# First feed-forward block: down products with the weights moving, output by token, turned back by 16 transposes

## The reference

```
def conv_ffn(xn, w_gate, conv_w, conv_b, w_up, w_down):
    S = xn.shape[1]
    g = xn @ w_gate
    gp = jnp.pad(g, ((0, 0), (CONV_WIDTH - 1, 0), (0, 0)))
    gc = conv_b + sum(conv_w[j] * gp[:, j:j + S] for j in range(CONV_WIDTH))
    h = jax.nn.gelu(gc, approximate=False) * (xn @ w_up)
    return h @ w_down
...
    for i in range(DEPTH):
        hn = rms_norm(h, norm_mix[i])
        ...
            mix = mla_mixer(hn, b_w_in[j], b_q_norm[j], b_w_uq[j], b_kv_norm[j], b_w_ukv[j], b_w_o[j], cos_r, sin_r)
        h = h + mix.astype(h.dtype)
        f = conv_ffn(rms_norm(h, norm_ffn[i]), ffn_w_gate[i], ffn_conv_w[i], ffn_conv_b[i], ffn_w_up[i], ffn_w_down[i])
        h = h + f.astype(h.dtype)
    return rms_norm(h, norm_final)
```

## Time and profile before

| | us |
|---|---|
| median of 3 runs (1070.09 to 1070.32) | 1070.15 |
| the profiled execution's own time | 1069.82 |
| its span | 1068.0 |
| PE busy in the span | 1059.3 (99%) |
| DVE, ACT, POOL busy | 746.9, 599.0, 142.3 |
| granted TensorE clock | 1.0 of full speed (2.4 GHz) throughout |

### The profile page before, as it was taken

The page is one execution under the profiler, slowest core; times in us unless marked ns, Lnnn a source line. Parts: engine busy times, 40 slices in busy tenths (PEclk is TensorE's granted clock), DMA queues, the critical chain, the costliest instruction groups (busy, mean ns, idle before and its releaser), DMA issues.

```text
span 1068.0 us, 18604 instructions
## 1 busy us (share of the span) xinstructions
PE 1059.3 (99%) x7388; PEld 911.8 (85%) x7388; DVE 746.9 (70%) x1274; ACT 599.0 (56%) x1021; POOL 142.3 (13%) x166
## 2 busy tenths in 40 slices
PE   9999999999999999999999999999999999999998
PEld 7887878656898999799999899899998798888886
DVE  5665565487555878868875887686777767777775
ACT  4532666544434567766565656555574556555464
POOL 0000010153110000623431100000022410000000
PEclk9999999999999999999999999999999999999999
DMA  9731121286613342056444364545542334544551
GB/s 384 321 140 64 74 79 40 89 287 219 223 53 119 125 156 86 2 198 228 157 168 138 139 227 168 197 160 196 180 175 98 141 119 157 198 175 186 212 184 52
DMA packets 25381, 168.69 MB, mean 158 GB/s; under 512 B 3280, under 2 KB 3536, under 8 KB 5456
## 3 DMA queue, kind: packets, MB, share of 16 engines
q1 hardware_dynamic: 25152, 167.25, 43.3%
q10 hardware_dynamic: 144, 0.26, 0.1%
HBM read 164.35 MB, written 1.05 MB: 155 GB/s over the span
## 4 chain that ended last, share of the span: by engine, by line
PE 97%; ACT 1%; DVE 1%; issue 0%; DVEq 0%; ACTq 0%
PE bank L438 19%; PE bank L440 18%; PE bank L439 18%; PE bank L444 15%; PE bank L445 8%; PE bank L1557 2%; PE bank L501 2%; PE bank L1721 2%; PE bank L1711 2%; PE bank L1701 1%; PE bank L1584 1%; PE bank L1575 1%; PE bank L453 1%; PE bank L2370 1%; PE bank L1402 1%; ACT TILE L1760 1%
## 5 line engine op out<-in xcount | busy, mean ns | idle before, releaser
L416 DVE TENSOR_TENSOR wlo<-raw,whi 128x1024 fp32r<-128x1024 f32 (+1 forms) x255 | 303.7, 1237 | 67.8 <-ACT whi L401 67.7
L438 PE MATMUL bank<-OPS,whi 128*128 128x256 f32 (+1 forms) x1012 | 320.1, 316 | 0.2
L440 PE MATMUL bank<-OPS,wlo 128*128 128x256 f32 (+1 forms) x1012 | 312.0, 308 | 0.0
L439 PE MATMUL bank<-OPS,whi 128*128 128x256 f32 (+1 forms) x1012 | 311.9, 308 | 0.0
L401 ACT ACTIVATE whi<-raw 128x1024 fp32r<-128x1024 f32 (+1 forms) x255 | 255.5, 1052 | 57.9 <-PE bank L440 55.4
L444 PE MATMUL bank<-OPS,whi 128*128 128x512 f32 x704 | 250.1, 399 | 0.2
L438 PEld LDWEIGHTS bank<-OPS,whi 128*128 128x128 f32 x1012 | 192.7, 190 | 17.1 <-issue 5.6
L440 PEld LDWEIGHTS bank<-OPS,wlo 128*128 128x128 f32 x1012 | 192.8, 191 | 9.8
L439 PEld LDWEIGHTS bank<-OPS,whi 128*128 128x128 f32 x1012 | 192.9, 191 | 9.6 <-issue 1.2
L445 PE MATMUL bank<-OPS,wlo 128*128 128x256 f32 x704 | 197.7, 281 | 0.0
L444 PEld LDWEIGHTS bank<-OPS,whi 128*128 128x128 f32 x704 | 132.3, 188 | 32.9 <-DVE FIRST L2599 0.8
(11 more groups left out here) (294 smaller groups left out, 1299.2 us busy)
## 6 DMA issues: line engine op xcount, KB each, us to landing
raw<-in_stream SPq DMA_DIRECT2D x143, 1024.0 KB, 4.9
PROJ<-in_stream SPq DMA_DIRECT2D x5, 1024.0 KB, 18.5
raw<-in_stream SPq DMA_DIRECT2D x4, 1056.0 KB, 8.5
PROJ<-PROJ SPq DMA_DIRECT2D x32, 64.0 KB, 3.7
FIRST<-in_first SPq DMA_DIRECT2D x1, 1248.0 KB, 5.5
C<-in_con SPq DMA_DIRECT2D x1, 1157.5 KB, 7.4
FIRST<-in_first SPq DMA_DIRECT2D x1, 1024.0 KB, 7.5
WST<-in_w_s SPq DMA_DIRECT2D x2, 256.0 KB, 7.8
```

What stands on the lines that cost most here:

```text
L416: nc.vector.tensor_tensor(c.w[1][:, part], c.raw[:, part], c.w[0][:, part].bitcast(F32), ALU.subtract).then_inc(*raises(c.lo[h]))
L438: nc.tensor.matmul(out, w[0], x[0], start=start, stop=False, skip_group_check=skip)
L439: nc.tensor.matmul(out, w[0], x[1], start=False, stop=False, skip_group_check=skip)
L440: return nc.tensor.matmul(out, w[1], x[0], start=False, stop=stop, skip_group_check=skip)
```

## The change

In block 0 `narrow` is gone, and `by_token` makes the down products there too: 24 matmuls of 512 columns per chunk in place of 48 of 256. Its banks are filled in the order 0, 2, 1, 3, without the opening transposes of X. The output now lies by token, and X by feature, so it has to be turned back. In `copy_rows` ScalarE copies each finished bank to SBUF (`rows_out`, four copies of 128 x 512). In `turn_rows` TensorE makes eight transposes of 128 x 128 from two of these copies into two of the banks; the first eight stand in down 10 ahead of its last bank, the other eight behind the first feature block of the latents (`amid`, called in `together` after k = 0). VectorE adds the turned banks to X, in pairs.

```diff
@@ Jobs.pe_step
                     for k in range(KD):
                         for j in i:
                             self.product.fill_part(e, self.product.jobs[j], (k,))
+                        if k == 0 and self.product.amid is not None:
+                            self.product.amid(e)
@@ ffn
-            def narrow(e, c, ch):
-                for point in due(e, ch.lo, ("h_hi_made", l, c), ("h_lo_made", l, c)):
-                    e.wait_ge(*point)
...
-                for f in range(KD):
-                    for t in range(2):
-
-                        mm = products(acc[f // 2].mem[:, (f % 2) * SEQ:(f % 2 + 1) * SEQ],
-                                      tuple(w[:, t * D + f * P:t * D + (f + 1) * P] for w in ch.w),
-                                      (HH[c % 2][:, t, :], HL[c % 2][:, t, :]),
-                                      c == 0 and t == 0 and f % 2 == 0, c == NF - 1 and t == 1, skip=True)
-                    if c == NF - 1 and f in (1, 3, 5):
-                        mm.then_inc(*raises(("sum_given", l, f // 2)))
-                mm.then_inc(*raises(ch.used))
+            rows_out = [PROJ[:, 512 * i:512 * i + 512] for i in range(4)]
+            pair_bank = [acc[2 * (m % 2) + m // 2] for m in range(4)]
+
+            def turn_rows(e, half):
+                for m in (2 * half, 2 * half + 1):
+                    for point in due(e, ("rows_copied", l, half), ("rows_copied", l, half + 2)):
+                        e.wait_ge(*point)
+                    for b in range(2):
+                        at = P * (2 * (m % 2) + b)
+                        for t in range(2):
+                            mm = nc.tensor.transpose(pair_bank[m].mem[:, b * SEQ + t * P:b * SEQ + t * P + P],
+                                                     rows_out[half + 2 * t][:, at:at + P], ident)
+                    mm.then_inc(*raises(("rows_turned", l, m)))
+
+            def copy_rows(e, i):
+                for point in due(e, given[i]):
+                    e.wait_ge(*point)
+                nc.scalar.activation(rows_out[i], acc[i].mem[:], ACT.Copy).then_inc(*raises(("rows_copied", l, i)))
@@ by_token
-                    for i, a in enumerate(acc):
+                    for i, a in enumerate(acc if l else ()):
...
-                for i, a in enumerate(acc):
+                for i in (0, 1, 2, 3) if l else (0, 2, 1, 3):
+                    a = acc[i]
+                    if l == 0 and c == NF - 1 and i == 3:
+                        turn_rows(e, 0)
@@ act of ffn
                 split_hi(e, by["down", NF - 1].s + 2.5)
+                for i in (0, 2, 1, 3) if l == 0 else ():
+                    copy_rows(e, i)
                 for i in range(1, 4 if l == 0 else 1):
                     s.gives.act(e, (2 * i - 2, 2 * i - 1))
@@ dve of ffn
-                for i, a in enumerate(acc if l == 0 else ()):
-                    for point in due(e, given[i]):
+                if l == 0:
+                    split_lo(e, by["down", NF - 1].s + 2.5)
+                for m, a in enumerate(pair_bank if l == 0 else ()):
+                    for point in due(e, ("rows_turned", l, m)):
                         e.wait_ge(*point)
-                    x = X[:, 2 * i:2 * i + 2, 0:SEQ]
+                    x = X[:, 2 * m:2 * m + 2, 0:SEQ]
                     nc.vector.tensor_tensor(x, two(a.mem), x, ALU.add).then_inc(*raises(a.read["dve"]))
-                    if i == 0:
-                        split_lo(e, by["down", NF - 1].s + 2.5)
-                    else:
-                        s.gives.dve(e, (2 * i - 2, 2 * i - 1))
-                    if i == 1:
+                    if m == 1:
+                        s.gives.dve(e, (0, 1))
                         split_lo(e, by["down", NF - 1].s + 3)
+                        s.gives.dve(e, (2, 3))
+                    if m == 3:
+                        s.gives.dve(e, (4, 5))
@@ program
         la = mla_latent(op1.block, high)
+        la.amid = ff.turn_rest
```

More of the change, by code:

```diff
@@ L1204, in dve @@
                         s.gives.dve(e, range(2 * i - 2 if i > s.begun else 0, 2 * i))
-            s.gives = s.after_act = None
+            s.gives = s.after_act = s.amid = None
             s.pe, s.act, s.dve = pe, act, dve
@@ L2875, in add_halves @@
                     *raises(("halves_summed", l, c, what)))
-            def narrow(e, c, ch):
-                for point in due(e, ch.lo, ("h_hi_made", l, c), ("h_lo_made", l, c)):
-                    e.wait_ge(*point)
-                if c == 0:
-                    for point in due(e, [a.empty for a in acc]):
-                        e.wait_ge(*point)
-                for f in range(KD):
-                    for t in range(2):
-                        mm = products(acc[f // 2].mem[:, (f % 2) * SEQ:(f % 2 + 1) * SEQ],
-                                      tuple(w[:, t * D + f * P:t * D + (f + 1) * P] for w in ch.w),
-                                      (HH[c % 2][:, t, :], HL[c % 2][:, t, :]),
-                                      c == 0 and t == 0 and f % 2 == 0, c == NF - 1 and t == 1, skip=True)
-                    if c == NF - 1 and f in (1, 3, 5):
-                        mm.then_inc(*raises(("sum_given", l, f // 2)))
-                mm.then_inc(*raises(ch.used))
+            rows_out = [PROJ[:, 512 * i:512 * i + 512] for i in range(4)]
[12 more added lines that the diff above has]
+                for point in due(e, given[i]):
+                    e.wait_ge(*point)
+                nc.scalar.activation(rows_out[i], acc[i].mem[:], ACT.Copy).then_inc(*raises(("rows_copied", l, i)))
             def by_token(e, c, ch):
@@ L2908, in by_token @@
                         w = tuple(w[:, at:at + 512] for w in ch.w)
-                        mm = products(a.mem[:], (HH[c % 2][:, t, tokens], HL[c % 2][:, t, tokens]), w, False,
-                                      c == NF - 1 and t == 1, skip=True)
+                        mm = products(a.mem[:], (HH[c % 2][:, t, tokens], HL[c % 2][:, t, tokens]), w,
+                                      l == 0 and c == 0 and t == 0, c == NF - 1 and t == 1, skip=True)
                     if c == NF - 1 and i < 3:
@@ L2937, in pe @@
                         wide(e, up[c], ch)
-                    elif l == 0:
-                        narrow(e, c, ch)
                     else:
@@ L3072, in ffn @@
             s.acc, s.given = acc, given
-            s.block = lambda k: acc[k // 2].freed
+            s.block = lambda k: pair_bank[k // 2].freed
+            s.turn_rest = lambda e: turn_rows(e, 1)
             s.used = [("down_added", l, NF - 1)]
```

## The result

| | before | with the change |
|---|---|---|
| median, us | 1070.16 (20 runs, 1069.87 to 1070.83) | 1071.62 (20 runs, 1071.18 to 1073.0) |
| ratio to before | | 1.0014 (95% interval 1.0008 to 1.0021) |
| span of the profiled execution, us | 1068.0 | 1069.4 |

The changed kernel is 1.46 us slower, 0.14%, which is clear of zero and under the 0.2% that the prediction calls no change. The forecast was +0.97.

A forecast was written before the change was run, and what follows sets the result against it. TensorE, 97% of the chain, was taken as the bound. The terms -2.86 - 0.10 + 1.87 + 1.94 + 0.12 gave +0.97 us, so 1071.1 us on the median, 0.09% slower; range 1069.1 to 1072.4.

The forecast's parts named there:

- if it waits again before their end: Sign of being wrong: TensorE, after the one wait ahead of the first latent matmul, waits again before the latents end.
- The products: Block 0's down stages fall from 5.76 to 5.50 us, 0.26 per chunk over 11 chunks: -2.86 us.
- gate and up: Block 0's gate and up stages, 11.31 us against block 1's 11.29: taken as -0.10 us, bounds -0.2 to 0.
- The transposes: Sixteen added on TensorE at 0.104 us each, 1.71, plus 0.16 for two slower first products: +1.87 us.
- Rival (c): Each of the 16 transposes costs its whole duration of 0.272 us: +2.64, or 1073.7 us; chance 2%.
- The new wait: TensorE idles ahead of the first latent matmul because ScalarE's high part queues behind all four copies: +1.94 us, bounds 0 to 2.3.
- rival (a): No wait ahead of the latents, whose first block is ready when down 10 ends: -0.97, or 1069.2 us; chance 8%.
- Down 10's start: From down 9 to down 10 in block 0, HL of chunk 10 comes late: +0.12 us, bounds -0.02 to +0.25.
- No second wait: Behind the latents' first feature block TensorE does not wait again, with about 2 us of slack: 0 us.
- rival (b): A second wait in the latents, at the fifth or seventh block, third job's weights late too: 1072.8 us with 1.7; chance 7%.

The follow-up runs named there:

- e5: Against the kernel before: down products by token alone, without copies or transposes, so X gets the rows in the wrong layout; 1067.41 us, ratio 0.9976.
- e4: Against the changed kernel: each of the 16 transposes done twice in a row into the same place; 1073.24 us, ratio to the kernel before 1.0030.
- e1: Against the changed kernel: ScalarE's fourth copy moved behind the high parts and squares of feature blocks 0 and 1; 1070.40 us, ratio to the kernel before 1.0003.
- e6: Against the kernel before: four unused ScalarE copies of 128 x 512 added ahead of the first high part, no transposes; 1073.42 us, ratio 1.0032.
- e7: Against the changed kernel: GpSimd's four sums of squares for the norm ahead of the latents cut to one column each; 1071.41 us, ratio to the kernel before 1.0015.
- e3: Against the changed kernel: second half of a weight chunk moved ahead of the copies and adds, fourth copy unmoved; 1071.25 us, ratio to the kernel before 1.0012.
- e2: Against e1: second half of a weight chunk also moved ahead of ScalarE's copies and VectorE's adds; 1069.81 us, ratio to the kernel before 0.9997.

## Why the prediction was right

The time and the large terms came out as forecast. One step of the mechanism did not, the one on a second wait, and the prediction's own sign of being wrong ("if it waits again before their end") is met there. The time stayed near the forecast because most of that wait was given back by a slack that the prediction had not priced, which is luck.

**The products** (forecast -2.86 and -0.10 for gate and up). The down stages are 5.50 us, as read. Up to the start of down 9 the profiled executions differ by 2.24, where 9 x 0.26 + 0.10 is 2.44; the first gate and up stage behind down 0 took 11.10 before and 11.29 after, which is that difference. e5, which has only this term and the late down 10, gained 2.67; the forecast for that pair was 2.86 + 0.10 - 0.12 = 2.84.

**The transposes** (forecast +1.87). Twice 0.79 and slower first steps of 0.08 are 1.74 in the trace, and e4 gives 0.101 to 0.112 for each. Rival (c) is out, and so is the Trainium skill's 275 ns ("TensorE: Matmul & The Clock Gate", Part 4) read as a price: the row's duration is 0.273 here too, and it doesn't add up.

**The new wait** (forecast +1.94). 1.93 us to the issue of the first latent product, and 0.08 in its first step, so 2.01. Its links were as read: the fourth copy starts 0.21 after the last bank is issued (773.41 to 773.62), the high part 0.49 later, the low part 0.60 later, TensorE 0.63 later. e1 and e6 show from both sides that ScalarE's order is the cause, and rival (a) is out.

**Down 10's start** (forecast +0.12, bounds -0.02 and +0.25). It was late by 0.32 in place of 0.05: +0.27, just over the upper bound. I had halved between block 0's 5.66 and block 1's 5.39 for HL; it was 5.68 (766.14 + 0.69 - 761.15). Block 0's own number was the one to take.

**No second wait** (forecast 0, rival (b) at 7%). This is the step that failed. Behind the first one the feature blocks came in time, as forecast. But there is a wait of 0.68 us at the third latent job, which needs both halves of its weights' low part; I had named that place only in the rival, and judged by the 7.9 us that the operand chain took before. From the first high part to the end of the last pair it was 774.11 to 783.85, 9.7 us, and not at most 8.8: VectorE's pair of low parts took 1.91 beside GpSimd, and the adds that ScalarE waits for stand behind it. In e7, with GpSimd's adds cut, the chain is 774.09 to 782.78, 8.7 us, as the forecast allowed. The weight halves stand behind the chain. They ended at 784.60 before, 2.04 us ahead of their need, if TensorE's start is 0.14 behind them; now they end 3.97 later (2.16 from the later start of the chain and 1.81 from its length), and TensorE wants them only 1.26 later. That sum was never made in the prediction. Of the 0.68 us, 0.52 was given back in the next stage, by the slack described at e3, and 0.11 was lost again behind it.

So the sum was 0.97. Against it the traces have +0.20 in products with gate and up, -0.13 in the transposes, +0.07 in the new wait, +0.15 at down 10 and +0.27 left of the second wait (0.68 - 0.52 + 0.11). That makes 1.53 at the first query product, 1.4 at the end of the span, and 1.46 between the medians.

## What to carry to other kernels

A change that saves the bound engine time in eleven regular stages can lose more than that at the one place where they end: trace the hand-over there link by link, in each engine's own queue order. A helper's instruction that waits for the last product must not stand ahead of what the next product needs, even if nobody waits for its result. Look, too, at what stands behind a chain that gets later and longer, and how much slack it has. And a helper's duration read where it runs alone does not hold beside another helper: take the row in which both run.

## What the runs showed of the hardware

VectorE's operations with two SBUF inputs ran slower beside a GpSimd add: 1.91 against 0.88 us for a pair of 128 x 256, 3.12 against 2.36 for a pair of 128 x 1024 (e7). One by one, in the changed kernel:

```profile
777.65 0.48 DVE L1050 SCALAR_TENSOR_TENSOR OPS<-FIRST,OPS 128x256 fp32r<-128x256 f32 x1
778.04 1.52 DVE L1050 SCALAR_TENSOR_TENSOR OPS<-FIRST,OPS 128x256 fp32r<-128x256 f32 x1
785.45 1.44 DVE L416 TENSOR_TENSOR wlo<-raw,whi 128x1024 fp32r<-128x1024 f32 x1 [1.02 <-ACT whi L401]
786.81 1.76 DVE L416 TENSOR_TENSOR wlo<-raw,whi 128x1024 fp32r<-128x1024 f32 x1
```

The first low part began ahead of GpSimd's add (777.93 to 779.27) and took its usual 0.48; the second took 1.52 and ended at 779.56, 0.29 after GpSimd. GpSimd is held up as well: its add of 128 x 256 at 785.89 took 1.60, where the same add takes 0.74 with VectorE idle (476.88 in the kernel before), and it ended at 787.49, 0.60 after VectorE's first half (786.89); VectorE's second half ended 1.08 after that. So in these rows the two take turns, each for a whole instruction. The adds of a bank to X, which have one input in SBUF, took the same 1.29 for two beside GpSimd (776.54 in e2, GpSimd from 776.53) as alone (771.78 in the change).

The Trainium skill, "SBUF — State Buffer", Who interferes with whom, has this as a port pair under an exclusive lock, over which a VectorE instruction with two SBUF inputs contends with a GpSimd instruction that reads SBUF. The trace agrees with it for these lines. The kernel before had it too, where it cost TensorE nothing:

```profile
776.11 1.67 DVE L1050 SCALAR_TENSOR_TENSOR OPS<-FIRST,OPS 128x256 fp32r<-128x256 f32 x2
781.45 3.15 DVE L416 TENSOR_TENSOR wlo<-raw,whi 128x1024 fp32r<-128x1024 f32 x2 [0.89 <-ACT whi L401]
```

In block 0's chunk 10 ScalarE takes up the gate's sum 3.90 us idle in place of 3.63 and so 0.27 late, in the kernel before, in the change and in e2 and e5, though its instruction waits for the same things as in the other chunks. What makes it late was not found.
